# Later row tiles held back until the first input weights have landed; the first projected tile's products interleaved with the turned fills

## What is computed

```python
def _modulate(x, cond, norm_g, w_ada, b_ada):
    mod = jax.nn.silu(cond) @ w_ada + b_ada
    shift, scale, gate = jnp.split(mod[:, None, :], 3, axis=-1)
    return rmsnorm(x, norm_g) * (1.0 + scale) + shift, gate
...
    h, gate = _modulate(x, c, norm_g, w_ada, b_ada)
    hc, gate_c = _modulate(xc, c_ctx[None, :], norm_g, w_ada, b_ada)
    qa, ka, va, qb, kb, vb, g = _split(h @ w_in, EVEN_SPLITS)
    qa = _rope(qa.reshape(B, S, A_HEADS, d), cos, sin).reshape(B, S, Hk, G, d)
```

## Time and profile before

| | us |
|---|---|
| median of the runs (lowest, highest) | 2830.58 (2827.45, 2832.51) |
| the profiled execution | 2830.81 |
| its span | 2829.0 |
| PE busy in it | 2726.1 (96%) |
| DVE, ACT, POOL busy | 1069.9, 785.7, 223.7 |
| granted clock of PE, mean | 0.992 of full speed |
| start to first product of the projection | 48.02 |

### The profile page before, as it was taken

The page is one execution under the profiler, slowest core; times in us unless marked ns, Lnnn a source line. Parts: engine busy times, 40 slices in busy tenths (PEclk is TensorE's granted clock), DMA queues, the critical chain, the costliest instruction groups (busy, mean ns, idle before and its releaser), DMA issues. The chain is left out here.

```text
span 2829.0 us, 32445 instructions
## 1 busy us (share of the span) xinstructions
PE 2726.1 (96%) x12154; PEld 1529.1 (54%) x12154; DVE 1069.9 (38%) x3023; ACT 785.7 (28%) x1684; POOL 223.7 (8%) x409
## 2 busy tenths in 40 slices
PE   5999999999999999999999999999999999999998
PEld 3477544477644445466745476444654465644443
DVE  3257521299712223344400174123833473212211
ACT  3136400277711112322200264112211462111100
POOL 2000000000000000000060030200000002012000
PEclk8999999999999999999999999999999999999999
DMA  7030000012011220211010001333220204134311
GB/s 261 7 109 32 20 30 30 30 68 72 34 65 65 79 86 19 93 38 38 12 54 30 30 22 42 86 83 119 96 71 30 71 16 133 67 119 168 133 60 45
DMA packets 71867, 188.46 MB, mean 67 GB/s; under 512 B 6844, under 2 KB 9600, under 8 KB 70784
## 3 DMA queue, kind: packets, MB, share of 16 engines
q0 software_dynamic: 27808, 99.04, 10.8%
q1 hardware_dynamic: 43152, 86.97, 8.9%
q10 hardware_dynamic: 752, 0.38, 0.0%
HBM read 143.69 MB, written 43.01 MB: 66 GB/s over the span
## 5 line engine op out<-in xcount | busy, mean ns | idle before, releaser
L1305 PE MATMUL psum<-RW,hT 128*128 128x512 f32 (+2 forms) x2208 | 926.2, 575 | 7.5 <-ACT hT L2197 4.7
L1305 PEld LDWEIGHTS psum<-RW,hT 128*128 128x128 f32 x2208 | 428.0, 198 | 434.8 <-issue 412.8
L1271 PE MATMUL psum<-RW,RQ 128*128 128x512 f32 x832 | 362.3, 594 | 1.1 <-ACT RQ L2234 1.1
L1341 PE MATMUL psum<-RQ 64*128 64x256 f32 (+5 forms) x1344 | 291.7, 492 | 2.3 <-DVE small L2038 1.5
L2383 ACT ACTIVATE RP<-RP,small 128x1280 f32<-128x1280 f32 (+11 forms) x274 | 252.0, 920 | 131.0 <-DVE small L2038 127.0
L2038 DVE CUSTOM_DVE_ANT_0 RP<-psum,small 128x512 f32<-128x512 f32 (+1 forms) x382 | 201.5, 574 | 178.5 <-PE psum L1341 89.7
L1271 PEld LDWEIGHTS psum<-RW,RQ 128*128 128x128 f32 x832 | 157.0, 191 | 191.4 <-issue 191.4
L1353 PE MATMUL psum<-ident,RP 128*128 128x128 f32 x1388 | 203.7, 281 | 9.8 <-DVE RP L2051 4.5
L2395 ACT ACTIVATE RP<-psum 128x512 f32<-128x512 f32 (+1 forms) x288 | 150.1, 521 | 192.0 <-PE psum L1353 180.3
L1353 PEld LDWEIGHTS psum<-ident,RP 128*128 128x128 f32 x1388 | 149.4, 141 | 81.7 <-issue 67.9
L1341 PEld LDWEIGHTS psum<-RQ 64*128 64x128 f32 (+1 forms) x1344 | 139.2, 186 | 90.4 <-issue 48.9
(11 more groups left out here) (321 smaller groups left out, 2284.3 us busy)
## 6 DMA issues: line engine op xcount, KB each, us to landing
RW<-in_w_in SPq DMA_DIRECT2D x7, 2048.0 KB, 8.1
RW<-in_ev_w_in SPq DMA_DIRECT2D x6, 2048.0 KB, 8.1
RW<-in_od_w_ada SPq DMA_DIRECT2D x6, 2048.0 KB, 7.9
RW<-in_od_w_in SPq DMA_DIRECT2D x5, 2048.0 KB, 7.9
RQ<-in_ev_w_ada SPq DMA_DIRECT2D x4, 2048.0 KB, 21.0
RX<-in_x POOLq DMA_DIRECT2D x16, 512.0 KB, 6.0
y_even<-YR POOLq DMA_DIRECT2D x20, 256.0 KB, 2.3
RP<-y_even POOLq DMA_DIRECT2D x20, 256.0 KB, 3.0
```

Source lines behind the costliest of these rows:

```text
L1271: last = pe.matmul(main.bank(f), yT[:, kk, :], w_buf(n)[:, kk, :], start=kk == 0, stop=kk == KC - 1)
L1305: last = pe.matmul(main.bank(f)[:, 0:nc_], lhs_of(st["lhs"], j["t"], kk), w, start=kk == 0, stop=kk == kn - 1)
L1341: last = pe.matmul(main.bank(f)[:, 0:pc["w"]], q, kk[:, keys], start=i == 0, stop=i == len(u["qk"]) - 1)
```

## The change

Four edits. POOL waits for the first input weights before it asks for row tile 4 (all later tiles are behind that on its queue). PE turns only the first two fills of group 0 ahead of the projection. In the projection of tile 0 every product waits for its own fill to be read out, and behind the products k = 0 to 5 stands the turning of fill k + 2. The wait of tile 0 for the whole of group 0 goes.

```diff
@@ -519,8 +519,9 @@
-                             jobs=turns_a, needs={0: gs[0], 4: gs[1], 8: gs[2]}),
+                             jobs=turns_a, needs={4: gs[1], 8: gs[2]}),
...
+        first_proj, first_rows = stages[-2], gs[0]
@@ -900,6 +901,8 @@
                         if j["x"] >= 3:
                             gp.wait_ge(s_xn, j["xn"] - 2)
+                        if t == 4:
+                            wait_weights(gp, first_proj["w"])
                         load_x(j, x[t * P:(t + 1) * P, :] if t < NT else ctx_in[(t - NT) * P:(t - NT + 1) * P, :])
@@ -1233,7 +1236,7 @@
                 elif k == "norm":
-                    turn_groups(st["jobs"])
+                    turn_groups(st["jobs"][:2])
@@ -1297,6 +1300,8 @@
                             w = w_buf(n)[:, kk, :]
+                            if st is first_proj and j["t"] == 0:
+                                turn.wait_drained(pe, first_rows["fills"][kk])
@@ -1304,6 +1309,8 @@
                                              start=kk == 0, stop=kk == kn - 1)
+                            if st is first_proj and j["t"] == 0 and kk + 2 < KC:
+                                turn_groups([(first_rows, kk + 2)])
                         main.written(last)
```

## The result

| | before | changed |
|---|---|---|
| median of 12 runs, us | 2831.34 | 2837.23 |
| lowest, highest | 2827.45, 2835.20 | 2834.06, 2840.01 |
| span of the profiled execution | 2829.0 | 2833.3 |

The ratio is 1.0019, with a 95% interval from 1.0011 to 1.0028: 5.4 us slower, with 3.1 to 7.9 in the interval. The ratio is worked out from all the runs and isn't the quotient of the two medians. That lies at the bound of 0.2% given in the prediction, and the interval doesn't take in "no change": the loss is small, but real. Applied to the 2830.58 of the three runs shown before, it is 2836.0, against a forecast of 2833.0 and inside the range of 2829.0 to 2837.0; the median of 2837.23 itself lies 0.2 above that range.

A forecast was written before the change was run, and what follows sets the result against it. PE's own queue was taken to set the time; +4.3 on the ACT chain, +0.2 turning and -2.15 half clock gave +2.35 on 2830.81, so 2833.2, and 2833.0 with the median 0.2 below; range 2829.0 to 2837.0.

The forecast's parts named there:

- Held-back rows: Row loads 4 to 6 behind ev_w_in: weights land 4.0 us earlier, at about 38.8 (bounds 38.8 and 42.8); no gain alone.
- row 3 doesn't come sooner: Start of the kernel: row 3's load gains 0 from rows 4 and 5 no longer being behind it.
- The chain through ACT: Group 0's last readout, then rows 4 to 9 and tile 0's rotation: all 4.3 us later; bounds 2.6 and 9.9.
- The restart: PE resuming before tile 2: already at half clock, turning 4.0 us, tile 2 loses 0.25 and ends at 79.4.
- half clock not paid again: Tile 2 after PE's wait: 2.15 us taken off, as its half-clock loss falls from 2.4 to 0.25.
- a difference behind 100 us: Sign of being wrong: any difference after the first 100 us, such as another clock level in the window attention.
- The late return of the clock: Rival, chance 0.17: full clock returns 4.8 us after tile 2's first product; tile 2 loses 2.4, +4.5, 2835.1.
- The weights were not late: Denies a rival, chance 0.10: ev_w_in keeps the first product waiting until 42.8; +2.9 in all, 2833.5.
- The slower rival: Chance 0.13: PE stays at half clock through all of tile 0, products standing between waits; +7.9, 2838.5.
- the step of 1.30 against a readout of 1.48 spread over 1.74: Tile 0: product plus fill takes 1.30 us; readout needs 1.48 of 1.74 available, so the new waits never bite.
- The faster rival: Chance 0.05: rows don't hold PE, if ACT reads row 4 before the last readout; -6.4, 2824.2.
- Same or slower: Whole-kernel verdicts against a 0.2% (5.7 us) bound: same 0.83, slower 0.13, faster 0.04.

## Why the prediction was right, and where its size was off

*Held-back rows: right, with the landing put too late.* They cost nothing by themselves and brought nothing by themselves (ratio 1.0003). Their effect on the weights was put at 4.0 us and was 3.8 to 5.4: 21.0 us from issue to landing with the loads held back, 24.8 in three profiles of before and 26.4 in one. The weights landed at 37.3, ahead of the 38.8 that was the early bound; the bytes of three row loads don't account for all of that, and what else does stays open. The gain has next to no use: with 24.8 the weights land at about 41.2, and the first product can't start ahead of 41.8; only the profile with 26.4 would have kept it waiting, 1 us. That row 3 doesn't come sooner held (27.26 instead of 27.40).

*The chain through ACT: right in mechanism and in size.* Predicted were 4.3 us from the later last readout to the first turned stage, with 2.6 as the lower bound if the clock didn't fall in tile 0. The means differ by 4.35, of which some 0.5 is the uneven draw of the clock in the fills; like with like it is 3.6 to 4.1. The first profile of the changed kernel, whose clock stayed at full there, is the low one with 26.2. In the second, whose clock fell at 42.2 and rose at 45.6, the steps came out as written: last fill at 51.16 (50.85 predicted), last readout ending at 52.58 (52.2), PE released at 68.71 (68.3), tile 2 done at 79.61 (79.4). PE's idle time was 7.6 to 8.1 (8.4).

*The restart: the mis-sized term, which was a gain that isn't there.* The prediction took 2.15 off, "half clock not paid again", because the one profile of before at hand paid 13.07 for this stretch. The other three paid 10.3. On the mean of four it is 11.0 before and 10.9 after, so the term is -0.1 and not -2.15 + 0.2. With it the prediction's own sum is +4.2 instead of +2.35, within the measured 3.1 to 7.9, and about 1 us short of the middle of it. The 0.9 behind tile 2 would close most of that, but a difference behind 100 us was named in the prediction as a sign of being wrong, and it isn't explained. A cost that one execution pays by chance was booked as one that each pays, and its removal as a gain.

*The rivals.* The late return of the clock didn't come: it was back 3.6 to 4.8 us after the restart in the four profiles of the changed kernel (4.5 predicted), while mostly transposes ran. The weights were not late in any of its profiles. The slower rival, half level through all of tile 0, didn't come either. The second profile of the changed kernel, us, PE PEld DVE ACT POOL busy, granted clock, DMA share, GB/s:

```profile
42.50:45.50 3.00, 3.00 (x8) 1.49 (x7) 0.69 (x1) 0.00 (x0) 0.00 (x0) 0.50 0.86 344
46.00:60.00 14.00, 13.99 (x48) 7.01 (x47) 3.88 (x5) 8.18 (x18) 2.31 (x5) 1.00 0.22 73
```

The Trainium skill's case for it (TensorE: Matmul & The Clock Gate, section HAM oscillation) needs real waits between the products, and here there were none, as the step of 1.30 against a readout of 1.48 spread over 1.74 had said. The faster rival was ruled out by ACT's order, and the kernels with rows 4 to 6 ahead show that it was that order: there PE stood no more and 2.8 and 3.1 us were won. That is half of the 6.4 named. The clock's 2.4 in it was there to be won in one execution of four only.

*Same or slower.* 0.83 was given to a change within 0.2%, and 0.19% was measured, with an interval that reaches past 0.2% on the slower side. That it came out below the bound and not above it is 0.3 us, which is luck; the size was more than twice the forecast. With the restart sized by its mean the forecast would have been 2834.8, and slower would have deserved more than 0.13.

## What to carry to other kernels

Before products are moved ahead of the transposes that feed them, look at what stands behind the last readout on the reading engine: here a chain of row tiles on ACT, of which PE waited already, was pushed back by twice what PE won. The idle time of the busiest engine names the engine whose order must change first; once rows 4 to 6 stood ahead of the readouts and the weights landed in time, the same interleaving cost nothing that the times show. And a stretch at half clock in a single profile should be taken as a chance of a cost: weigh it by how often it comes in several executions before it is put into a sum.

## What was not expected of the hardware

The granted clock behind a wait of 1.56 to 2.14 us fell in one execution of four (2.00) and stayed at 2.4 GHz in three, with the same instructions and nearly the same times. One such fall cost 2.8 us, half of what this change is worth.

The landing of ev_w_in took 21.0 us from its issue where no row load behind row 3 ran on POOL's queue meanwhile, 24.8 or 26.4 with rows 4 to 6 in flight, and 28.4 with rows 4 to 8. The Trainium skill (DMA: Bandwidth & Descriptors, section Issuing engines are not separate DMA queues) says that loads started by different engines run on the same 16 DMA engines and interleave, and the traces agree.
